# Attention's gate weights split by VectorE and ScalarE, with the low halves summed by a transfer from GpSimd's queue

## What is computed

```
proj = u @ w_in                      # xp | q | k | v | gate_logits (2 x 1024 columns)
z = q k^T / 8 ; beta = sigmoid(z)
A[t,s] = beta[t,s] * prod_{s<j<t} (1 - beta[t,j])      # strictly causal, 8 heads of 64
o_sb = A v ; y_sb = o_sb @ w_branch_attn
g = sigmoid(gate_logits)
h = h + (g_pool * y_pool + g_sb * y_sb) @ w_out
```

## Time and profile before

| | us |
|---|---|
| median of 3 runs | 1924.63 (1923.79 to 1924.8) |
| the profiled execution, its own time | 1924.49 |
| its span (first to last instruction) | 1922.5 |
| TensorE busy in the span | 1911.0 |
| VectorE busy | 1392.9 |
| ScalarE busy | 786.7 |
| GpSimd busy | 152.1 |

### The profile page before, as it was taken

The page is one execution under the profiler, slowest core; times in us unless marked ns, Lnnn a source line. Parts: engine busy times, 40 slices in busy tenths (PEclk is TensorE's granted clock), DMA queues, the critical chain, the costliest instruction groups (busy, mean ns, idle before and its releaser), DMA issues.

```text
span 1922.5 us, 25204 instructions
## 1 busy us (share of the span) xinstructions
PE 1911.0 (99%) x9046; PEld 1599.3 (83%) x9046; DVE 1392.9 (72%) x1714; ACT 786.7 (41%) x1170; POOL 152.1 (8%) x221
## 2 busy tenths in 40 slices
PE   9999999999999999999999999999999999999998
PEld 9888888888888888888888888898888888888886
DVE  6977867774566776786878878879777777755655
ACT  7423232323434543345665652464323232334344
POOL 1000000000000300002443420010000000000002
PEclk9999999999999999999999999999999999999999
DMA  5456654558676534248446347643545444677665
GB/s 165 147 198 228 225 174 149 189 196 312 210 236 196 185 110 151 73 134 236 142 127 175 105 154 254 191 136 114 182 141 197 148 168 153 220 265 240 204 195 200
DMA packets 246723, 347.19 MB, mean 181 GB/s; under 512 B 16368, under 2 KB 150256, under 8 KB 243056
## 3 DMA queue, kind: packets, MB, share of 16 engines
q1 hardware_dynamic: 246640, 346.10, 55.3%
HBM read 232.79 MB, written 112.98 MB: 180 GB/s over the span
## 4 chain that ended last, share of the span: by engine, by line
PE 95%; DVE 2%; DMA 1%; ACT 1%; issue 1%; POOL 1%; SPq 0%; POOLq 0%; DVEq 0%; ACTq 0%
PE bank L1233 39%; PE bank L1330 10%; PE bank L1277 8%; PE bank L1278 8%; PE bank L1279 8%; PE bank L1187 5%; PE bank L1471 4%; PE bank L1379 2%; PE bank L1407 2%; PE bank L1437 2%; PE bank L1543 2%; PE bank L1162 1%; PE bank L1562 1%; PE bank L1561 1%; PE bank L1528 1%; PE bank L1526 1%
## 5 line engine op out<-in xcount | busy, mean ns | idle before, releaser
L2171 DVE TENSOR_TENSOR dn_lo<-dn_lo_raw,dn_hi 128x1024 fp32r<-128x1024 f32 x149 | 181.9, 1223 | 150.9 <-ACT dn_hi L1741 150.5
L1233 PE MATMUL bank<-lo_t,wa_hi 128*128 128x512 f32 x640 | 249.0, 389 | 0.0
L1233 PE MATMUL bank<-hi_t,wa_hi 128*128 128x512 f32 x640 | 249.0, 389 | 0.0
L1233 PE MATMUL bank<-hi_t,wa_lo 128*128 128x512 f32 x640 | 249.0, 389 | 0.0
L1741 ACT ACTIVATE dn_hi<-dn_lo_raw 128x1024 fp32r<-128x1024 f32 x149 | 157.9, 1060 | 219.3 <-DMA dn_lo_raw<-act_dram 219.3
L1277 PE MATMUL bank<-dn_hi 128*128 128x512 f32 x596 | 232.5, 390 | 0.0
L1279 PE MATMUL bank<-dn_lo,dn_hi 128*128 128x512 f32 x596 | 231.9, 389 | 0.0
L1278 PE MATMUL bank<-dn_hi,dn_lo 128*128 128x512 f32 x596 | 231.9, 389 | 0.0
L1233 PE MATMUL bank<-hi_b,wa_hi 128*128 128x512 f32 x480 | 186.9, 389 | 0.9 <-DVE up L2295 0.9
L1233 PE MATMUL bank<-lo_b,wa_hi 128*128 128x512 f32 x480 | 186.8, 389 | 0.0
L1233 PE MATMUL bank<-hi_b,wa_lo 128*128 128x512 f32 x480 | 186.7, 389 | 0.0
(11 more groups left out here) (275 smaller groups left out, 3764.1 us busy)
## 6 DMA issues: line engine op xcount, KB each, us to landing
wa_lo_raw<-in_ffn_w_gate_up_dram SPq DMA_DIRECT2D x87, 512.0 KB, 4.9
dn_lo_raw<-act_dram SPq DMA_DIRECT2D x149, 256.0 KB, 4.3
act_dram<-g SPq DMA_DIRECT2D x44, 512.0 KB, 4.3
wd_t<-in_ffn_w_down_dram SPq DMA_DIRECT2D x44, 512.0 KB, 6.6
act_dram<-s_of SPq DMA_DIRECT2D x88, 256.0 KB, 6.4
wd_dram<-wd_t SPq DMA_DIRECT2D x22, 1024.0 KB, 5.9
dn_lo_raw<-wd_dram SPq DMA_DIRECT2D x85, 256.0 KB, 3.4
dn_lo_raw<-in_ffn_w_down_dram SPq DMA_DIRECT2D x64, 256.0 KB, 3.1
```

Source lines behind the costliest of these rows:

```text
L1233: last = nc.tensor.matmul(acc, lhs, rhs, start=n == 0 and i != 2 and i < 5, stop=n == 11, skip_group_check=True)
L2171: return nc.vector.tensor_tensor(dst, raw, hi.bitcast(f32), ALU.subtract)
```

## The change

VectorE and ScalarE change places, and a transfer does the subtraction. VectorE writes `w_hi` as a copy of `w_raw` that rounds, in step s. ScalarE writes the negative of `w_hi` into `w_lo`, at the end of step s+1. At the start of its step s+2, where s is the step of a unit's last piece, GpSimd waits for ScalarE's last piece (`whi`) and issues one transfer for the whole unit that adds `w_raw` to `w_lo` (SBUF to SBUF, 1 MB, `accum_op=ALU.add`). A new semaphore `wsum` counts 16 for each landed transfer. TensorE waits for `wsum` ahead of the first matmul that reads `w_lo` of units 1 to 7, and SP, which now loads a step later (s+3), waits for it before it overwrites `w_raw`. Unit 0 and the units before and after attention are split as before; `lows_before` maps their counts. `wghi` and `wglo` become one semaphore `wg_split`, in another stage, with the same instructions.

```diff
+def lows_before(g):
+    return min(g, U_GATE + 1) + max(g - U_C, 0)
...
@@ unit (SP)
                 if gg >= 2:
                     sp_.wait_ge(whi, gg - 1)
-                    sp_.wait_ge(wlo, gg - 1)
+                    if U_GATE < gg - 2 < U_C:
+                        sp_.wait_ge(wsum, 16 * (gg - 2 - U_GATE))
+                    else:
+                        sp_.wait_ge(wlo, lows_before(gg - 1))
...
-                    for j, piece in PIECES_AT[s - 2] if s > 1 else ():
+                    for j, piece in PIECES_AT[s - 3] if s > 2 else ():
                         if piece == PIECES - 1 and j + 2 < NG:
                             gate_unit(j + 2)
...
@@ gate_parts (TensorE)
                     if m == 2 and fb == GATE_FIRST[j]:
-                        pe.wait_ge(wlo, U_GATE + j + 1)
+                        if j:
+                            pe.wait_ge(wsum, 16 * j)
+                        else:
+                            pe.wait_ge(wlo, U_GATE + 1)
...
@@ split_piece (ScalarE)
-                if piece == 0:
-                    act.wait_ge(raw_in[par], 32 * ((U_GATE + j) // 2 + 1))
-                    if j >= 2:
-                        act.wait_ge(gate_ready, GATE_LAST[j - 2] + 1)
-                    else:
-                        act.wait_ge(acc_ready, 4 * Q_GATE)
+                act.wait_ge(wpiece, PIECES * (j - 1) + piece + 1)
                 ab, kts = 2 * piece // PIECES, slice(KT // 2 * (piece % 2), KT // 2 * (piece % 2 + 1))
-                nc.scalar.activation(w_hi[:, par, ab, kts, :], w_raw[:, par, ab, kts, :],
-                                     ACT.Copy).then_inc(whi if piece == PIECES - 1 else wpiece, 1)
+                last = nc.scalar.activation(w_lo[:, par, ab, kts, :], w_hi[:, par, ab, kts, :].bitcast(f32), ACT.Copy, scale=-1.0)
+                if piece == PIECES - 1:
+                    last.then_inc(whi, 1)
...
-                for j, piece in PIECES_AT[s]:
+                for j, piece in PIECES_AT[s - 1] if s else ():
                     split_piece(j, piece)
...
@@ split_piece (VectorE)
-                if piece < PIECES - 1:
-                    dve.wait_ge(wpiece, (PIECES - 1) * (j - 1) + piece + 1)
-                else:
-                    dve.wait_ge(whi, U_GATE + j + 1)
+                if piece == 0:
+                    dve.wait_ge(raw_in[par], 32 * ((U_GATE + j) // 2 + 1))
+                    if j >= 2:
+                        dve.wait_ge(gate_ready, GATE_LAST[j - 2] + 1)
+                    else:
+                        dve.wait_ge(acc_ready, 4 * Q_GATE)
                 ab, kts = 2 * piece // PIECES, slice(KT // 2 * (piece % 2), KT // 2 * (piece % 2 + 1))
-                last = nc.vector.tensor_tensor(flat(w_lo[:, par, ab, kts, :]), flat(w_raw[:, par, ab, kts, :]),
-                                               flat(w_hi[:, par, ab, kts, :]).bitcast(f32), ALU.subtract)
-                if piece == PIECES - 1:
-                    last.then_inc(wlo, 1)
+                nc.vector.tensor_copy(flat(w_hi[:, par, ab, kts, :]), flat(w_raw[:, par, ab, kts, :])).then_inc(wpiece, 1)
...
@@ GpSimd, new
+            def add_weights(j):
+                par = j % 2
+                pool.wait_ge(whi, U_GATE + j + 1)
+                if j > 1:
+                    pool.wait_ge(wsum, 16 * (j - 1))
+                nc.gpsimd.dma_start(w_lo[:, par].rearrange("p a k f -> p (a k f)").bitcast(f32),
+                                    w_raw[:, par].rearrange("p a k f -> p (a k f)"), accum_op=ALU.add).then_inc(wsum, 16)
+
             for s in range(NA + DRAIN):
+                for j, piece in PIECES_AT[s - 2] if s >= 2 else ():
+                    if piece == PIECES - 1:
+                        add_weights(j)
                 if s < NA:
                     mask_diagonal(s)
```

More of the change, by code:

```diff
@@ L460, in macaron_layer @@
         wpiece = sem("wpiece")
-        wghi = sem("wghi")
-        wglo = sem("wglo")
+        wsum = sem("wsum")
+        wg_split = sem("wg_split")
         mb_in = sem("mb_in")
@@ L1027, in load_branch_unit @@
                 sp_.wait_ge(whi, g - 1)
-                sp_.wait_ge(wlo, g - 1)
+                if n < 2:
+                    sp_.wait_ge(wsum, 16 * (g - 2 - U_GATE))
+                else:
+                    sp_.wait_ge(wlo, lows_before(g - 1))
                 for k in range(0, BR, 2):
@@ L1104, in _ @@
             sp_.wait_ge(whi, U_C + 1)
-            sp_.wait_ge(wlo, U_C + 1)
+            sp_.wait_ge(wlo, lows_before(U_C + 1))
             for b in range(2):
@@ L1388, in group_quad @@
                 pe.wait_ge(ylo, 2 * m + 2)
-                pe.wait_ge(wglo, 1)
+                pe.wait_ge(wg_split, 2)
                 for b in range(4):
@@ L1591, in branch_tile @@
                 pe.wait_ge(whi, U_C + j + 1)
-                pe.wait_ge(wlo, U_C + j + 1)
+                pe.wait_ge(wlo, lows_before(U_C + j + 1))
                 for th in (1, 0) if j == 0 else (0, 1):
@@ L2028, in _ @@
             act.wait_ge(mb_add, 5 * NM)
-            nc.scalar.activation(wg_hi[:, :, :], wg_raw[:, :, :], ACT.Copy).then_inc(wghi, 1)
+            nc.scalar.activation(wg_hi[:, :, :], wg_raw[:, :, :], ACT.Copy).then_inc(wg_split, 1)
             pool_hi(0, 1)
@@ L2706, in group_weights_lo @@
             def group_weights_lo():
-                dve.wait_ge(wghi, 1)
+                dve.wait_ge(wg_split, 1)
                 nc.vector.tensor_tensor(wg_lo[:, :, :].rearrange("p g d -> p (g d)"),
@@ L2711, in group_weights_lo @@
                                         wg_hi[:, :, :].rearrange("p g d -> p (g d)").bitcast(f32),
-                                        ALU.subtract).then_inc(wglo, 1)
+                                        ALU.subtract).then_inc(wg_split, 1)
             def pool_weight_sums(u):
@@ L2903, in _ @@
                     turned_lo(s - 2)
-                for j, piece in PIECES_AT[s - 1] if s else ():
+                for j, piece in PIECES_AT[s]:
                     split_piece(j, piece)
```

## The result

The changed kernel takes 1966.06 us (median of 4 runs, 1965.15 to 1966.88), the kernel before, run on the same chip, 1924.51 us: a ratio of 1.0216, with a 95% interval of 1.0203 to 1.0228. It is 41.5 us slower. The profiled execution took 1965.15 us and its span is 1963.2 us, 40.7 more than the span of before. The lines named here have moved by 11 to 16: the gate products (L1330 before) are L1343 now, the turning of tiles (L1543) is L1559, GpSimd's product with the pooled branch is L3052, its masks L3044, and the new transfer L3060.

The account below looks back on a forecast made before the run. TensorE was taken to bound the kernel: seven waits on a 10.0 us transfer, 7 x 10.19 - 31.44 = 39.9 us, added to 1924.49 give 1964.4, forecast as 1964.5 us; range 1936 to 2006 us.

Parts of the forecast that it names:

- little lost to the clock: Main forecast for TensorE's waits on w_lo: transfer of 8 to 12 us, 1950 to 1979 us, chance 0.45.
- the rival of the falling clock: TensorE's clock falls after stalls of 4 us or more: 8 to 15 us on top, 1973 to 1980, chance 0.13.
- TensorE bounds the stretch and nothing else does: From 876 to 1152 us TensorE is busy 274.72 of 276.00 us; relieving other engines gives at most 1.3 us.
- VectorE and ScalarE cost nothing: Exchanged splitting work in attention: VectorE regains 0 to 9.6 us busy time, ScalarE nothing; taken as 0 at the end.
- When each is issued: GpSimd issues units 1 to 6 behind the pooled-branch product, 897.41 to 1083.53 us, and unit 7 at 1100.70.
- Margins: Time from GpSimd's issue to the first matmul on w_lo: 2.03 to 6.29 us per unit, in sum 31.44.
- How long the transfer takes: Adding transfer of 1 MB from issue to landing: 10.0 us, bounds 6.0 and 15.8; stalls in sum 39.9 us.
- the rival of the cheap second read: Adding transfer takes 5.1 to 8 us like plain ones: 1931.6 to 1950.5 us, chance 0.24.
- The clock: TensorE's clock behind the seven stalls: nothing taken in the forecast; a possible 2.1 us for each of four to seven stalls.
- the masks behind GpSimd's issue: GpSimd's masks, queued after the issue, were costed at nothing, since stalls of over 3 us cover an issue 3 us longer.
- three signs that would have proved me wrong: In TensorE's profile: waits of equal length, waits at L1559, or matmuls 0.43 us apart instead of 0.23 behind a stall.
- the signs of being right: Seven TensorE waits at L1343 of 4 to 8 us, longest at unit 6, busy time unchanged, issues behind the pooled-branch product.

Follow-up runs that it names:

- both early forms: Changed kernel with weight pieces and transfer issued earlier: 1924.91 us; changed kernel with each 1 MB transfer cut into two of 512 KB: 1924.67 us.
- the copying kernel: Changed kernel whose transfer from GpSimd's queue copies the raw weights over the negatives instead of adding: 1938.42 us, ratio 1.0069.

## Why the prediction was right, and where it was not

I forecast 1964.5 us and it is 1966.06. The sign, the place and the waits are as I said. But the number is closer than its terms: one was too large and one was missing, and that the two nearly cancel is luck. The time fell into the range of the forecast, "little lost to the clock", while what happened is the rival of the falling clock, with a shorter T.

- **TensorE bounds the stretch and nothing else does.** Right, and now shown from three sides: without waits on the transfer the time is that of before (ratios 1.0004 and 1.0000); 9.0 us more of work on VectorE cost nothing (1.0001); later issues are paid one for one.
- **VectorE and ScalarE cost nothing.** Right. VectorE's rounding took 418 ns in the median, between my bounds of 340 and 683, ScalarE's negation 652 ns for the 648 that I took, and VectorE got back 8.2 us, of at most 9.6, for nothing at the end.
- **When each is issued.** Right. Unit 1 was issued at 897.81 for the 897.41 of the forecast, behind the product with the pooled branch. Margins, as the time to the released product less the stall, came to 33.5 us in sum for 31.44.
- **How long the transfer takes.** The step was right in kind and mis-sized. I took 2.0 + 2 x 4.0 = 10.0 us. The median is 8.4. The plain part of the sum, 6.0, is about right (the copy takes 5.8), but the addition puts 2.6 us on top of it and not 4.0. From issue to product the seven took 61.0 us where the forecast had 7 x 10.19 = 71.3. With the margins that makes stalls of 27.5 us instead of 39.9, 12.4 too many. I had taken the value at which both operands are moved in full one after the other; the rival of the cheap second read (T of 5.1 to 8) named the better direction, but even its upper end was passed, and T = 8.4 lies in my forecast's own span of 8 to 12.
- **The clock.** The step that failed: I left the loss at nothing in the forecast and made it a rival with a chance of 0.13, 2.1 us for each of four to seven stalls. It happened, behind six of seven, and cost 13.6 us of busy time, 2.3 apiece. The price from the start of the program is near that mean, though the single losses run from 1.5 to 3.0 us and the granted clock was given as full at the start, so that the two need not be the same thing. The forecast took nothing because the waits of the trace before were too short to tell; that no row speaks for a cost is no reason to put it at nothing. The rival's condition, a stall of 4 us or more, was wrong too: three of the six waits were of about 3 us. By the Trainium skill, TensorE: Matmul & The Clock Gate, Part 1, an idle TensorE falls to 1.2 GHz and has to be busy for a while to come back. The traces agree: a granted clock of 0.70 to 0.86 in the ten microseconds behind six waits of 2.9 to 5.5 us, and 1.00 behind unit 6 where the wait was filled with products.
- **The rest.** The waits before turned tiles grew from 1.3 to 1.7 us, so the masks behind GpSimd's issue cost nothing to speak of. Of the three signs that would have proved me wrong, waits of equal length did not come (2.65 to 5.53 us), nor more waits at L1559 to speak of, but products spaced at 0.42 instead of 0.23 us did. Of the signs of being right, busy time unchanged failed (13.6 us more), five of the seven waits were shorter than 4 us, and the issue follows the product with the pooled branch in six units, as the forecast's own sum had it. The longest wait was at unit 6, as forecast (5.53 us), though unit 4's 5.15 is close, since that transfer was the slowest and not only its margin short.

Put right, the sum reads 1924.49 + 27.5 + 13.6 = 1965.6, for 1965.15 of the profiled execution. Had the two terms been taken at their measured sizes apart, the forecast would have been 1952 without the clock and 1978 with the clock and my T, wrong by 14 and by 12 us. That is the measure of how well I knew it.

The Trainium skill's estimate for the transfer, from DMA: Bandwidth & Descriptors, Anatomy of one DMA, was 4.4 us with the bytes counted once and 6.8 with them counted twice. The copy from GpSimd took 4.6 us at its fastest and 5.8 in the median, the addition 6.9 and 8.4. So the two estimates come near the fastest transfers, on DMA engines that had other work for more than half of the time, and the medians are 1.4 to 1.6 us above.

## What to carry to other kernels

A transfer that takes the place of an engine's work takes none of that engine's time, but it has a latency that the work did not have, here 8.4 us against the 0.7 of VectorE's last subtraction. Before putting one in, list for each use the time between its earliest issue and its need, and move the issue ahead by the slowest landing, not by the median; then it is free, as both early forms showed. Where TensorE is the bound, price every stall of about 2.5 us or more at its length plus some 2 us for the clock behind it (1.5 to 3.0 here). And an engine's relief is worth only what the bound engine waits for it: 8.2 us off VectorE were worth nothing here.

## What was not expected of the hardware

- The clock does not follow the length of the idle time alone. It fell behind waits of 2.52, 2.56, 2.83 and 2.93 us and all longer ones of these runs, but not behind one of 2.65 us in the changed kernel (1.00 in the window after it) nor behind one of 1.67 us in the copying kernel. What else decides between 2.5 and 2.8 us is open.
- The fall need not come at the wait's end. Behind the last wait of the changed kernel (3.19 us) the products first follow at 0.12 us and only a microsecond later at 0.21:

```profile
1144.24 0.50 PE L1343 MATMUL bank<-u_hi,w_lo 128*128 128x512 f32 x1 [3.19 <-DMA w_lo<-w_raw]
1144.58 0.28 PE L1577 MATMUL bank<-at_hi,v_w 128*128 128x256 f32 x1
1144.70 0.28 PE L1578 MATMUL bank<-at_lo,v_w 128*128 128x256 f32 x1
...
1145.57 0.42 PE L1578 MATMUL bank<-at_lo,v_w 128*128 128x256 f32 x1
1145.78 0.41 PE L1577 MATMUL bank<-at_hi,v_w 128*128 128x256 f32 x1
```

- What the clock costs does not follow the wait's length either. Waits of 44.5 us in sum went with 15.6 us of slower products, waits of 26.4 us with 13.6. Single waits, each with TensorE's loss behind it against the same products of the kernel before: 3.06, 2.93, 5.15, 3.90, 5.53 and 3.19 us were followed by losses of 1.5, 1.6, 2.4, 2.9, 3.0 and 1.7 us; in the kernel with the later issue 4.77, 5.30, 9.41, 6.14, 4.60, 6.23 and 8.02 us by 2.3, 2.5, 1.7, 1.8, 2.2, 2.3 and 2.6. The longest wait has one of the smallest losses.
- An adding transfer of 1 MB takes 1.4 to 1.5 times as long as a copy (8.4 against 5.8 us in the median, 6.9 against 4.6 at the fastest) and not twice as long, and its issue holds GpSimd for 0.87 us where a copy's takes 0.60 and ScalarE's 0.47.
